# Hybrid S5 and sparse-attention decoder step: where the squares of x are added up and where the root is made

## What is computed

```python
def rmsnorm(x, g):
    xf = x.astype(jnp.float32)
    y = xf * lax.rsqrt(jnp.mean(xf * xf, axis=-1, keepdims=True) + EPS)
    return (y * g.astype(jnp.float32)).astype(x.dtype)

def trunk_layer(x, ...):
    xn = rmsnorm(x, norm_mix)
    proj = xn @ w_in
    ...                                   # index scores, attention, S5 scan, gates
    x = x + merged.astype(x.dtype) @ w_out
    hn = rmsnorm(x, norm_ffn)
    gate, up = jnp.split(hn @ w_ffn_up, 2, axis=-1)
    x = x + (jax.nn.silu(gate) * up) @ w_ffn_down
```

## Time and profile before

| | |
|---|---|
| median of 3 runs | 3553.61 us (3552.67 to 3554.78) |
| the profiled execution | 3560.83 us |
| its span, first to last instruction | 3559.0 us |
| mean granted TensorE clock | 0.961 |
| busy: TensorE, VectorE, ScalarE, GpSimd | 3409.2, 1598.4, 918.5, 220.1 us |
| HBM | 149 GB/s over the span |

### The profile page before, as it was taken

One profiled execution on the slowest core, in us unless ns is written; L12 is line 12 of the kernel. 1 busy time (PEld: TensorE's weight loads), 2 busy tenths in 40 slices (PEclk: granted clock), 3 DMA queues, 4 the chain that ended last, 5 costly groups with the idle time before them and its releaser, 6 DMA issues.

```text
span 3559.0 us, 55669 instructions
## 1 busy us (share of the span) xinstructions
PE 3409.2 (96%) x21390; PEld 3093.5 (87%) x21390; DVE 1598.4 (45%) x2970; ACT 918.5 (26%) x1348; POOL 220.1 (6%) x232
## 2 busy tenths in 40 slices
PE   7999889999999999999989998899999999999999
PEld 5778768788899999999977786687888999999998
DVE  2136758211245544555421277581011555455553
ACT  1011131110045433333311211311100444333332
POOL 3230000120000000000032200001100000000000
PEclk9989989998999999999999899899899999999999
DMA  5433314443455554555444333245334655556553
GB/s 176 144 121 106 110 62 134 157 158 96 141 181 181 179 191 163 181 181 190 137 160 132 115 120 105 68 130 178 124 117 137 186 182 185 182 165 181 181 191 138
DMA packets 142191, 530.80 MB, mean 149 GB/s; under 512 B 19424, under 2 KB 20576, under 8 KB 141184
## 3 DMA queue, kind: packets, MB, share of 16 engines
q1 hardware_dynamic: 132512, 503.03, 44.3%
q0 software_dynamic: 9216, 25.18, 2.1%
q10 hardware_dynamic: 352, 1.11, 0.1%
HBM read 524.20 MB, written 5.05 MB: 149 GB/s over the span
## 4 chain that ended last, share of the span: by engine, by line
PE 47%; DVE 1%; ACT 1%; issue 1%; DMA 0%; ACTq 0%; DVEq 0%; SPq 0%
PE main L412 11%; PE main L780 7%; PE main L782 7%; PE main L781 7%; PE main L436 4%; PE main L560 3%; PE main L753 3%; PE side L731 1%; PE side L532 1%; PE side L513 1%; PE side L696 0%; PE side L443 0%; DVE tmp L1080 0%; PE side L543 0%; PE side L685 0%
## 5 line engine op out<-in xcount | busy, mean ns | idle before, releaser
L1376 DVE TENSOR_TENSOR w_ffn_low<-ring,w_ffn_high 128x1024 fp32r<-128x1024 f32 (+1 forms) x480 | 638.7, 1331 | 487.7 <-ACT w_ffn_high L989 487.0
L780 PE MATMUL main<-x_ffn_high,w_ffn_high 128*128 128x264 f32 x2816 | 800.5, 284 | 1.3 <-issue 1.3
L781 PE MATMUL main<-x_ffn_low,w_ffn_high 128*128 128x264 f32 x2816 | 799.1, 284 | 0.0
L782 PE MATMUL main<-x_ffn_high,w_ffn_low 128*128 128x264 f32 x2816 | 798.7, 284 | 0.0
L989 ACT ACTIVATE w_ffn_high<-ring 128x1024 fp32r<-128x1024 f32 (+1 forms) x480 | 549.2, 1144 | 729.0 <-PE main L782 719.3
L780 PEld LDWEIGHTS main<-x_ffn_high,w_ffn_high 128*128 128x128 f32 x2816 | 531.8, 189 | 2.1 <-issue 2.1
L781 PEld LDWEIGHTS main<-x_ffn_low,w_ffn_high 128*128 128x128 f32 x2816 | 532.2, 189 | 0.0
L782 PEld LDWEIGHTS main<-x_ffn_high,w_ffn_low 128*128 128x128 f32 x2816 | 529.3, 188 | 0.0
L412 PE MATMUL main<-xn,ring 128*128 128x264 f32 x2112 | 485.8, 393 | 7.1 <-DVE xn L1016 7.1
L412 PEld LDWEIGHTS main<-xn,ring 128*128 128x128 f32 x2112 | 408.9, 194 | 81.9 <-issue 10.0
L780 PE MATMUL main<-hidden_high,w_ffn_high 128*128 128x264 f32 x1408 | 402.4, 286 | 9.1 <-DVE hidden_low L1400 9.1
(11 more groups left out here) (293 smaller groups left out, 2755.1 us busy)
## 6 DMA issues: line engine op xcount, KB each, us to landing
ring<-in_w_up SPq DMA_DIRECT2D x352, 512.0 KB
ring<-in_w_in SPq DMA_DIRECT2D x264, 512.0 KB
ring<-in_w_down SPq DMA_DIRECT2D x128, 704.0 KB
ring<-in_w_br SPq DMA_DIRECT2D x64, 512.0 KB
ring<-in_w_out SPq DMA_DIRECT2D x64, 512.0 KB
ring<-in_w_glu SPq DMA_DIRECT2D x16, 512.0 KB
x<-in_x SPq DMA_DIRECT2D x1, 2112.0 KB, 8.1
out_x<-x SPq DMA_DIRECT2D x1, 2112.0 KB, 6.4
```

The costliest lines, as they stand in the source:

```text
L780: mm(out, wfh[:, slot, w], high[:, kk, :], start=kk == 0, stop=False)
L781: mm(out, wfh[:, slot, w], low[:, kk, :], start=False, stop=False)
L782: m = mm(out, wfl[:, slot, w], high[:, kk, :], start=False, stop=kk == chunks * kts - 1)
L1376: tt(wfl[:, s, 0:cols], ring[:, s, 0:cols], wfh[:, s, 0:cols].bitcast(F32), ALU.subtract).then_inc(low_ready, 1)
```

## The change

- For the FFN's norm ScalarE still squares slice after slice, but GpSimd adds the squares into a new tile `sqsum` as they come (`sq_added`). TensorE multiplies `sqsum` by the ones once, behind block 0 of the first up phase (`sq_summed`), and ScalarE's root waits for that.
- In the last down phase ScalarE's `finish` waits for each residual add, squares the slice into a quarter of `tmp`, and GpSimd adds (`last_sq`, `last_added`). Behind the last block TensorE sums over the partitions once, ScalarE takes the root and VectorE the reciprocal, within the same layer. The next layer's VectorE begins with the normalized slices.
- Layer 0's root is made ahead of the loop, in the opening block, with 16 squares and 16 summing matmuls as before; the barrier of that block follows.
- gn is loaded in the opening block, and for the next layer in the FFN, after `xf_ready` has reached 16. Each layer issues five tensors ahead of its weights and not six. The host arranges gn so that entry l holds what is needed from the FFN of layer l - 1 on.
- The second layer makes a root too, which nothing reads.

```diff
+        sqsum = sb("sqsum", [P, T])
...
                 sp.dma_start(consts[:], d["consts"]).then_inc(consts_in, 16)
+                sp.dma_start(gn[:], d["gn"][0]).then_inc(consts_in, 16)
...
+            @block.scalar
+            def _(act):
+                act.wait_ge(consts_in, 96)
+                act.wait_ge(consts_made, 1)
+                for k in range(NT):
+                    if k >= 2:
+                        act.wait_ge(sq_used, k - 1)
+                    nc.scalar.activation(sq[:, k % 2, :], x[:, k, :], ACT.Square).then_inc(sq_ready, 1)
+                act.wait_ge(sq_used, NT)
+                nc.scalar.activation(rs[:, 0, :], side[3][:, 0:T], ACT.Sqrt, bias=small[:, 7:8], scale=1.0 / DM).then_inc(std_ready, 1)
...
                 def _(sp):
 
-                    sp.dma_start(gn[:], d["gn"][layer]).then_inc(params_in, 16)
                     sp.dma_start(gqk[:], d["gqk"][layer]).then_inc(params_in, 16)
...
                                 load(src, s, s, cols)
+                            sp.wait_ge(xf_ready, NT)
+                            sp.dma_start(gn[:], d["gn"][layer + 1]).then_inc(gn_in, 16)
...
-                    for k in range(NT):
-                        pe.wait_ge(sq_ready, k + 1)
-                        mm(side[3][:, 0:T], ones, sq[:, k % 2, :], start=k == 0, stop=k == NT - 1).then_inc(sq_used, 1)
                     blocks(0, 1, 0, 2, 8, lambda k: xn[:, k, :], xn_ready)
...
                                 m.then_inc(units, 1)
-                            if not first or s:
-                                sum_square(i, s - 1, start=first and s == 1)
...
                             body(0, 0, 1, True)
+                            pe.wait_ge(sq_added, NT)
+                            mm(side[3][:, 0:T], ones, sqsum[:], start=True, stop=True).then_inc(sq_summed, 1)
                             body(0, 1, 3)
...
+                    pe.wait_ge(last_added, 4 + NT)
+                    mm(side[3][:, 0:T], ones, sqsum[:], start=True, stop=True).then_inc(last_summed, 1)
...
                     def finish(i, s, up, half, n0, seq0):
+                        if not up and half == 1 and s % 2 == 1:
+                            m = s // 2
+                            act.wait_ge(resid, i * 4 + (2 * NT + m + 1))
+                            act.wait_ge(last_added, i * 4 + (m + 1))
+                            af(tmp[:, m * T:(m + 1) * T].unsqueeze(1), x[:, bass.ds(i * 4 + m, 1), :], ACT.Square).then_inc(last_sq, 1)
...
                     ffn_steps(act, high, finish)
+                    act.wait_ge(last_summed, 1)
+                    af(rs[:, 0, :], side[3][:, 0:T], ACT.Sqrt, bias=small[:, 7:8], scale=1.0 / DM).then_inc(last_std, 1)
...
-                    dve.wait_ge(std_ready, 1)
-                    st.link(v.reciprocal(rs[:, 0, :], rs[:, 0, :]))
-                    dve.wait_ge(params_in, 96)
                     for k in range(NT):
                         stt(xn[:, k, :], x[:, k, :], gn[:, 0, k:k + 1], rs[:, 0, :], ALU.mult, ALU.mult).then_inc(xn_ready, 1)
...
                     ffn_steps(dve, low, finish)
+                    dve.wait_ge(last_std, 1)
+                    st.link(v.reciprocal(rs[:, 0, :], rs[:, 0, :]))
...
+                    for k in range(NT):
+                        pool.wait_ge(sq_ready, k + 1)
+                        if k == 0:
+                            g.tensor_copy(sqsum[:], sq[:, 0, :]).then_inc(sq_added, 1)
+                        else:
+                            pool.wait_ge(sq_added, k)
+                            g.tensor_tensor(sqsum[:], sqsum[:], sq[:, k % 2, :], ALU.add).then_inc(sq_added, 1)
+                    pool.wait_ge(sq_summed, 1)
+                    pool.sem_inc(last_added, 4)
+                    for k in range(NT):
+                        made = tmp[:, k % 4 * T:(k % 4 + 1) * T]
+                        pool.wait_ge(last_sq, k + 1)
+                        if k == 0:
+                            g.tensor_copy(sqsum[:], made).then_inc(last_added, 1)
+                        else:
+                            pool.wait_ge(last_added, 4 + k)
+                            g.tensor_tensor(sqsum[:], sqsum[:], made, ALU.add).then_inc(last_added, 1)
```

More of the change, by code:

```diff
@@ L321, in _ @@
                 st = Steps(pool, pool_step)
-                pool.wait_ge(consts_in, 80)
+                nc.gpsimd.memset(small[:], EPS).then_inc(consts_made, 1)
+                pool.wait_ge(consts_in, 96)
                 st.link(nc.gpsimd.iota(kix, pattern=[[0, 4 * NPAGES]], base=0, channel_multiplier=1))
@@ L335, in _ @@
                 st.link(nc.gpsimd.memset(qb[:], 0.0))
-                st.link(nc.gpsimd.memset(small[:], EPS))
+            @block.scalar
[8 more added lines that the diff above has]
+                nc.scalar.activation(rs[:, 0, :], side[3][:, 0:T], ACT.Sqrt, bias=small[:, 7:8], scale=1.0 / DM).then_inc(std_ready, 1)
+            @block.tensor
+            def _(pe):
+                for k in range(NT):
+                    pe.wait_ge(sq_ready, k + 1)
+                    nc.tensor.matmul(side[3][:, 0:T], ones, sq[:, k % 2, :], start=k == 0, stop=k == NT - 1).then_inc(sq_used, 1)
+            @block.vector
+            def _(dve):
+                dve.wait_ge(std_ready, 1)
+                nc.vector.reciprocal(rs[:, 0, :], rs[:, 0, :]).then_inc(last_std, 1)
+                dve.wait_ge(last_std, 1)
         nc.all_engine_barrier(sems_to_clear=range(cleared[0], cleared[-1] + 1))
@@ L737, in _, with out_blocks @@
                     pe.wait_ge(merged, 32)
[L739 to L744, removed]
+                    def out_blocks(i):
                         for s in range(4):
@@ L755, in out_blocks @@
                                 m.then_inc(units, 1)
[L756 to L762 removed]
+                    with pe.Fori(0, NT // 4) as i:
+                        out_blocks(i)
                     def split_blocks(first, n0, count, chunks, kts, high, low, wait_k):
@@ L833, in evac_gates, with norm @@
                         evac(first, count, 2 * first + 2, 2, lambda j: gates[:, bass.ds(j + (first - GL), 1), :], ACT.Tanh, 0.5)
-                    def norm(n, beside=None):
+                    def norm(beside):
                         for k in range(NT):
-                            if beside and k == NT - 1:
+                            if k == NT - 1:
                                 beside()
-                            if k >= 2 or n:
-                                act.wait_ge(sq_used, NT * n + k - 1)
-                            if n:
-                                act.wait_ge(resid, k + 1)
+                            if k >= 2:
+                                act.wait_ge(sq_added, k - 1)
+                            act.wait_ge(resid, k + 1)
                             af(sq[:, k % 2, :], x[:, k, :], ACT.Square).then_inc(sq_ready, 1)
-                        act.wait_ge(sq_used, NT * (n + 1))
-                        if n:
-                            act.wait_ge(xn_ready, NT)
+                        act.wait_ge(sq_summed, 1)
+                        act.wait_ge(xn_ready, NT)
                         af(rs[:, 0, :], side[3][:, 0:T], ACT.Sqrt, bias=small[:, 7:8], scale=1.0 / DM).then_inc(std_ready, 1)
-                    norm(0)
-                    act.wait_ge(params_in, 96)
-                    act.wait_ge(std_ready, 1)
+                    act.wait_ge(params_in, 80)
                     af(disc[:, 0, :], ssmp[:, 2, :], ACT.Exp).then_inc(expdt, 1)
```

16 lines of the change are left out of this document (9 added, 7 removed).

## The result

The changed kernel took 3564.47 us (median of 9 runs, 3563.17 to 3566.42), the kernel before 3554.75 us (9 runs, 3552.67 to 3558.67). The ratio is 1.0026, with a 95% interval of 1.0017 to 1.0035: 9.7 us slower, where 5.5 us less was forecast.

What follows compares the result with a forecast made beforehand. The prediction took TensorE, its matmul part busy for 96% of the span, as the bound. Terms -13.5 + 4.0 - 4.6 + 3.5 + 0.6 + 4.5 = -5.5 us took the median 3553.6 to 3548.1 us, range 3541 to 3557.

Steps and rivals of the forecast that it cites:

- Part 4: Layer boundary: norm chain reaches the barrier 4.5 us later, but TensorE then waits only for the first weights: -4.6 us.
- part 6: Tail: the second layer's unused root and its chain stand ahead of the final barrier and store of x: +4.5 us.
- Part 1: Output projection: 15 sums of 0.45 us leave TensorE in each of 2 layers: -13.5 us.
- Rival D: Output projection held to 7.57 us by something else, such as ring loads or residual adds: 3561.6 us, chance 0.06.
- Part 2: FFN opening: later root, 1.5 us stall and 0.45 us sum, 2.0 us in each layer: +4.0 us.
- rival B: FFN opening costs more: GpSimd excludes VectorE (+1.5), half-speed spell behind the new gap (2 x 1.7); 3553.0 us, chance 0.15.
- Part 3: Last down phase: 16 squares and adds delay the high parts by 1.1 us, covered by slack; priced at nothing.
- rival C: Last down phase's splits can't keep up, 16 squares a layer delay TensorE 1.1 us each: 3583 us, chance 0.04.
- Part 5: Launch: norm moves ahead of the barrier, so weights load later and TensorE starts at 38.6, not 35.12: +3.5 us.
- clock allowance: Launch and layer boundary: lower clock may last longer after over 10 us of idle TensorE, 0.3 us each: +0.6 us.
- rival A: Openings cost less: FFN stall hidden by lower clock, first weights land 8.7 us behind SyncE's first issue; 3542.8 us, chance 0.25.

Runs made afterwards that it cites:

- e1: The kernel before, unchanged, profiled a second time: 3553.21 us, span 3551.4.
- e9: The kernel after, unchanged, measured again on a third chip: 3563.33 us beside 3554.15 of the kernel before, ratio 1.0024.
- e10: The kernel before with only the FFN norm's squares added on GpSimd and its summing matmul ahead of FFN block 0: 3545.90 us, ratio 0.9977.
- e11: Kernel after with early GpSimd drain, last square on TensorE, FFN sum before block 0, first weights loaded before the barrier (launch's after x), signalled first: 3531.73 us, ratio 0.9935.
- e3: The kernel after with an added GpSimd drain behind its gathers and small operations, ahead of the adds: 3552.66 us, ratio 0.9996 to the kernel before.
- e5: The kernel after with the FFN norm's summing matmul ahead of FFN block 0 instead of behind it: 3563.92 us beside 3562.44 of the kernel before, ratio 1.0005.
- e2: The kernel before with GpSimd's last small operation of each layer held back until the last residual add: 3573.17 us, ratio 1.0053.
- e12: The kernel after with four GpSimd drains in each layer, behind gathers and small operations: 3561.18 us beside 3561.70, one run of each.
- e4: The kernel after with the last down phase's last square summed straight on TensorE, without a GpSimd add: 3551.89 us, ratio 0.9993 to the kernel before.

## Why the prediction was wrong

The table is worked out from the traces: the start of the same TensorE matmul in each kernel, minus its start in e1, at the edges of the stages (us). It shows where each one loses or gains.

| | e9 (after) | e10 | e11 |
|---|---|---|---|
| first matmul of layer 0 | +3.47 | -0.19 | -4.84 |
| into the output projection | +3.59 | -0.02 | -4.32 |
| its last block | -2.64 | -6.25 | -10.55 |
| start of FFN block 0 | -2.09 | -5.70 | -9.98 |
| 36 matmuls on | -0.56 | -4.17 | -8.65 |
| block 1, behind the stall | +1.46 | -4.17 | -8.65 |
| last matmuls of layer 0 | -0.07 | -4.15 | -8.70 |
| first matmul of layer 1 | +1.34 | -3.52 | -19.55 |
| into its output projection | +1.26 | -3.41 | -21.20 |
| its last block | -4.97 | -9.64 | -27.43 |
| block 1, behind the stall | -1.08 | -7.56 | -25.59 |
| last matmul | +0.33 | -7.54 | -25.70 |
| end of the span | +9.4 | -7.5 | -21.5 |

**Part 4 and part 6, the barrier: the step that failed.** "Barrier 2.04" was taken from the kernel before and put behind the new chain as if it were a constant. The chain was right: 4.4 us at both ends (4.5 forecast). But the 2.04 held only as all other engines had arrived long before. The change gives GpSimd work behind its gathers, and I priced that work alone ("nothing is queued behind it on GpSimd"). The barrier's own drain is queued behind it. The barrier opens 4.7 us behind VectorE's arrival in place of 0.2 (0.2 both in the kernel before and in e3), so 2 x 4.55 = 9.1 us. At the boundary the forecast -4.6 became +0.1 in the first trace and +1.4 in e9; at the end of the span the forecast +4.5 became +9.1. SyncE's first issue comes 11.05 us behind the last residual add, where the prediction named 6.5 to 7 as a sign. None of its three signs of being wrong appeared (gaps in the last down phase, openings released by VectorE, another output pace): none of them looked at the barrier. With the drain moved (e3) both ends came out as forecast: in its trace the boundary gave 4.2, and the end of the span cost 4.5.

**Part 1, the output projection.** -6.23 a layer instead of -6.75. The prediction counted 15 sums between the blocks, but there are 14: the 15th also runs in the pause ahead of the FFN. -12.5 in place of -13.5, and the pace of 7.12 as forecast. Rival D is out.

**Part 2, the FFN opening.** The sum and the stall were 2.02 us a layer against 2.0 forecast, with the queue that the text named; e5 took it away whole. Two smaller terms had been set to nothing. First, VectorE beside GpSimd: a subtraction that takes 0.43 us alone took 0.86 beside a GpSimd add (the row of 2758.94 above), and three splits took 4.03 in place of 3.49, so that block 0 starts 0.55 later a layer. It is rival B's first half, bounded at 0.74 us a layer and priced at nothing. The Trainium skill (SBUF — State Buffer, "Who interferes with whom") says that the two share a port pair which one holds at a time; the 0.43 to 0.86 agrees. By that rule the forecast would have been up to 1.5 us higher, and the traces show 1.1. Second, the half-speed spell in block 0, 1.3 to 1.5 us a layer. I took it for a fixture, since the profiled kernel before had it in both layers; e1 has it in neither, e2 in one, and every kernel here that sums squares on GpSimd in both. Why it does is open: no experiment separated the longer pause ahead of block 0 from the rest. With squares summed between the blocks, that pause is 3.40 us in every layer (start of the last output matmul to block 0), and the spell comes in some layers (both of the first profile, one of e2) and not in others (e1, the other of e2); with GpSimd adding, the pause is 3.94 and the spell is always there. The new gap of 1.3 us behind block 0 brought no spell, as forecast.

**Part 3, the last down phase.** Nothing, as forecast: between block 1 and the last matmul e9 gains 1.5 us on e1 in one layer and loses 1.4 in the other, where rival C's price was 17.6 us a layer. And TensorE's idle time in the down phases is 9.1 us in the kernel after as in e1. Groups of the kernel after, matmuls of both down phases (busy, mean ns, idle before):

```profile
L795 PE MATMUL main<-hidden_high,w_ffn_high 128*128 128x264 f32 x1408 | 402.5, 286 | 9.1 <-DVE hidden_low L1419 9.1
```

C is out.

**Part 5, the launch.** 38.2 against 38.6 forecast, released by the DMA, as said: +3.47 against 3.5, without the clock allowance of 0.3 at this place. TensorE starts 8.8 us behind SyncE's first issue here and 10.07 at the boundary, near the forecast's 8.7 and 10.3. So rival A is out too: its boundary at 8.7 didn't come, and the stall of part 2 wasn't hidden.

In sum, from -5.5: +9.1 for the drain, +1.1 for the slower VectorE, +2.8 for the spells in block 0, +1.0 for the miscounted sums, -0.6 for the allowance: +7.9, against 9.7 by the medians and 9.4 by the spans of e1 and e9. Most of the remaining 1.5 to 1.8 lies at e9's boundary, which is 1.3 us above that of the first trace: TensorE starts 11.35 us behind SyncE's first issue there. SyncE issues the first weight unit 3.50 us behind its first load, against 3.15 in the first trace, and takes 3.71 for the four units against 1.88; why isn't shown. Two single steps in FFN stages which nobody edited (-1.53 and +1.41) cancel.

Without the drain the other terms add up to -1.2 us, and e3, which takes only the drain away, measured -1.4 (-4.6 to +1.8) by its ratio. The range was missed by the drain alone: without its 9.1 us the time would have been inside. But the forecast's -5.5 would not have been met, and the centre was off by these smaller terms too.

## What to carry to other kernels

Before you give an engine new work at the end of a stage, look at what it did before and what it still owes: list the instructions of the barrier on every queue, drains too, and ask of each what it hides behind now. A barrier's price in one kernel is the price for its arrival order; if the order changes, work it out anew from each engine's last instruction. And if an engine must be late, let it settle its debt early: one drain of its own behind the gathers gave 11 us here.

If a norm leaves a barrier with nothing but a load behind it, move the load ahead of the barrier too, behind what is needed sooner, with its signal first in the queue. That, with the earlier sum of the FFN norm and e4's last square on TensorE, is what e11 has over e3: 0.0061 of the time.

## What the runs showed of the hardware

- A drain of GpSimd behind gathers (indirect DMAs) takes, counted from the end of GpSimd's last work, 1.9 to 2.2 us behind one, 3.9 behind 32, 5.4 behind 63 (e12) and 7.89 behind 96 (e3). The 7.89 were the same where the last gather was 1000 us old (e2). Behind plain operations it takes 0.05 us (e12).
- An added drain on an engine with time to spare costs nothing measurable (e3).
- A VectorE subtraction of two 264-column operands takes 0.86 us beside a GpSimd add, 0.43 alone (kernels after and before, layer 1).
- On ScalarE the root stands straight behind its table load, as it did in the earlier trace rows: in e11 the load starts at 1770.13, takes 1.28, and the root starts at 1771.43.
- The same kernel, unchanged, takes 3554 us on two chips and 3562 us on a third. In two executions of it that are 7.6 us apart, most of the difference lies in one stage of each layer, with 0.52 against 0.66 granted over 25 us in layer 0.
